# Low parts of weight tiles made by a negated copy on ScalarE and an adding DMA, in place of a subtraction on GpSimd

## What is computed

```python
def sq_relu_mlp(h, w_up, w_down):
    return jnp.square(jax.nn.relu(h @ w_up)) @ w_down

def swiglu(x, w_gate, w_up, w_down):
    return (jax.nn.silu(x @ w_gate) * (x @ w_up)) @ w_down
```

## Time and profile before

| | |
|---|---|
| time, median of 3 runs | 2312.11 us (2310.51 to 2312.12) |
| time of the profiled execution | 2310.62 us |
| its span | 2308.8 us |
| instructions | 29435 |
| granted TensorE clock | 0.999 |
| busy: PE, PEld | 99%, 82% of the span |
| busy: DVE, ACT, POOL | 46%, 44%, 58% |
| data moved by DMA | 213.74 MB, mean 93 GB/s |
| last chain, by engine | PE 91%, DVE 4%, POOL 2%, ACT 2%, issue 1% |

### The profile page before, as it was taken

The page is one execution under the profiler, slowest core; times in us unless marked ns, Lnnn a source line. Parts: engine busy times, 40 slices in busy tenths (PEclk is TensorE's granted clock), DMA queues, the critical chain, the costliest instruction groups (busy, mean ns, idle before and its releaser), DMA issues.

```text
span 2308.8 us, 29435 instructions
## 1 busy us (share of the span) xinstructions
PE 2287.9 (99%) x11249; PEld 1886.6 (82%) x11253; DVE 1064.7 (46%) x1428; ACT 1015.3 (44%) x1961; POOL 1335.8 (58%) x1008
## 2 busy tenths in 40 slices
PE   9999999999999999999999999999999999999998
PEld 8888888778878888788887888888898778888887
DVE  3423457544474656634546322434242564142534
ACT  4524444444674444443446233334333662333342
POOL 5533687783535778774354355768454503566773
PEclk9999999999999999999999999999999999999999
DMA  6321432322303243133330362331333202613222
GB/s 189 90 60 60 151 113 65 101 87 69 101 24 131 102 123 105 47 110 89 94 87 27 98 192 74 96 105 55 101 105 81 75 2 88 204 54 112 81 83 73
DMA packets 156947, 213.74 MB, mean 93 GB/s; under 512 B 33615, under 2 KB 81479, under 8 KB 156807
## 3 DMA queue, kind: packets, MB, share of 16 engines
q1 hardware_dynamic: 153424, 203.24, 29.4%
q10 hardware_dynamic: 3383, 8.62, 1.2%
HBM read 209.18 MB, written 2.10 MB: 92 GB/s over the span
## 4 chain that ended last, share of the span: by engine, by line
PE 91%; DVE 4%; POOL 2%; ACT 2%; issue 1%; DMA 0%; SPq 0%; DVEq 0%; ACTq 0%; POOLq 0%
PE PS L369 25%; PE PS L371 20%; PE PS L957 7%; PE PS L958 7%; PE PS L956 7%; PE PS L995 5%; PE PS L994 5%; PE PS L993 5%; PE PS L1944 2%; POOL WL L345 1%; PE PS L1922 1%; PE PS L489 1%; PE PS L2849 1%; DVE X L620 1%; ACT JUNK L578 1%
## 5 line engine op out<-in xcount | busy, mean ns | idle before, releaser
L345 POOL TENSOR_TENSOR WL<-WS,WH 128x512 fp32r<-128x512 f32 (+1 forms) x644 | 887.8, 1393 | 657.1 <-ACT WH L333 619.6
L333 ACT ACTIVATE WH<-WS 128x512 fp32r<-128x512 f32 (+2 forms) x606 | 373.8, 624 | 787.0 <-PE PS L369 283.2
L345 POOL TENSOR_TENSOR WL<-h_R,WH 128x512 fp32r<-128x512 f32 x240 | 348.6, 1473 | 115.1 <-ACT WH L330 112.2
L369 PE MATMUL PS<-AH,WH 128*128 128x512 f32 (+1 forms) x1072 | 324.0, 355 | 1.2 <-ACT AH L506 1.2
L369 PE MATMUL PS<-AL,WH 128*128 128x512 f32 (+1 forms) x1072 | 319.9, 352 | 0.5 <-DVE AL L524 0.3
L369 PE MATMUL PS<-AH,WL 128*128 128x512 f32 x880 | 313.2, 390 | 0.0
L956 PE MATMUL PS<-AH,WH 128*128 128x512 f32 x704 | 274.4, 390 | 0.6 <-POOL WL L345 0.6
L957 PE MATMUL PS<-AL,WH 128*128 128x512 f32 x704 | 274.6, 390 | 0.0
L958 PE MATMUL PS<-AH,WL 128*128 128x512 f32 x704 | 274.6, 390 | 0.0
L330 ACT ACTIVATE WH<-h_R 128x512 fp32r<-128x512 f32 x240 | 148.8, 631 | 244.3 <-PE PS L995 96.8
L371 PE MATMUL PS<-WH,AH 128*128 128x512 f32 (+1 forms) x552 | 214.9, 395 | 0.5 <-POOL WL L345 0.5
(11 more groups left out here) (419 smaller groups left out, 3647.1 us busy)
## 6 DMA issues: line engine op xcount, KB each, us to landing
WS<-in_mlp_w_up_dram SPq DMA_DIRECT2D x128, 256.0 KB, 3.1
h_R<-in_mlp_w_down_dram SPq DMA_DIRECT2D x96, 256.0 KB, 3.2
WS<-in_ffn_w_gate_dram SPq DMA_DIRECT2D x176, 128.0 KB, 2.2
WS<-in_ffn_w_up_dram SPq DMA_DIRECT2D x176, 128.0 KB, 2.2
h_R<-in_ffn_w_down_dram SPq DMA_DIRECT2D x64, 256.0 KB, 3.2
WS<-in_gla_w_in_dram SPq DMA_DIRECT2D x48, 256.0 KB, 2.7
WS<-in_even_w_in_dram SPq DMA_DIRECT2D x48, 256.0 KB, 2.6
WS<-in_mlp_w_down_dram SPq DMA_DIRECT2D x32, 256.0 KB, 2.8
```

The lines of the kernel that those rows point to most:

```text
L333: e.activation(WH[:, s, 0:n], WS[:, s, 0:n], ACT.Copy).then_inc(hi.sem, hi.tick(i))
L345: e.tensor_tensor(WL[:, s, 0:n], source, WH[:, s, 0:n].bitcast(F32), ALU.subtract).then_inc(lo.sem, lo.tick(i))
L369: return e.matmul(PS[b][0:mw, cs], weight[:, s, m * mw:(m + 1) * mw], x[:, cs], start=start, stop=stop, skip_group_check=head is not None)
```

## The change

For tiles of p1, p2 and p3 (`BY_DMA`) POOL no longer subtracts. ACT writes the tile twice: the rounded part into WH, and the same rounded part with a scale of -1 into WL. Then POOL, waiting for the second copy, issues a DMA that adds the raw tile in `hR` onto that slot of WL. Its landing is counted on one of six new semaphores (`rested`), and everybody who waited for `lo` of such a tile now waits for that: TensorE, SP's next load into the slot and its reload of the raw tile, and DVE where it overwrites a raw block or a WS slot. `rest(i)` picks the semaphore. The diff, with the places left out where only `w.wait_ge(lo, ...)` became `w.wait_ge(*rest(...))`:

```diff
+        rested = [Sig(ctx.enter_context(nc.semaphore(f"weight_rest_summed{i}"))) for i in range(NS)]
...
+        by_dma = set()
...
+        def rest(i):
+            return (rested[i % NS], i) if i in by_dma else (lo, i)
 
         def weight_in(e, w, i):
             if i >= len(stream):
                 return
             if i >= NS:
-                w.wait_ge(lo, i - NS)
+                w.wait_ge(*rest(i - NS))
...
                 source, *at = mixed[i]
                 w.wait_ge(*at)
                 e.activation(WH[:, s, 0:n], source, ACT.Copy).then_inc(hi.sem, hi.tick(i))
+                if i in by_dma:
+                    e.activation(WL[:, s, 0:n], source, ACT.Copy, scale=-1.0).then_inc(sc.sem, sc.tick("less", i))
                 return
...
             n, s = width(i), i % NS
+            if i in by_dma:
+                w.wait_ge(sc, "less", i)
+                e.dma_start(WL[:, s, 0:n], mixed[i][0], accum_op=ALU.add).then_inc(
+                    rested[s].sem, rested[s].tick(i, by=16))
+                return
             w.wait_ge(hi, i)
...
+        BY_DMA = ("p1", "p2", "p3")
...
             if c:
-                w.wait_ge(lo, first[D.name, c - 1, ("p4", "p5", "p2", "p3")[b]] + k)
+                w.wait_ge(*rest(first[D.name, c - 1, ("p4", "p5", "p2", "p3")[b]] + k))
...
                     mixed[i0 + k] = weight_source(D, c, p, k, i0 + k)
+                    if p in BY_DMA:
+                        by_dma.add(i0 + k)
...
                 s = (i0 + k) % NS
-                w.wait_ge(lo, i0 + k)
+                w.wait_ge(*rest(i0 + k))
```

More of the change, by code:

```diff
@@ L259, in program @@
         stored = Sig(ctx.enter_context(nc.semaphore("stored")))
-        sigs = [mm, sc, ve, po, hi, lo, stored, *landed, *ld.values(), *itertools.chain(*raw)]
+        sigs = [mm, sc, ve, po, hi, lo, stored, *landed, *rested, *ld.values(), *itertools.chain(*raw)]
         BA, BB = [0, 1, 2, 3], [4, 5, 6, 7]
@@ L409, in gemm @@
                 for kc in range(HEAD):
-                    w.wait_ge(lo, i0 + kc)
+                    w.wait_ge(*rest(i0 + kc))
                     for m in range(count(kc)):
@@ L462, in narrow @@
             i = first[name]
-            w.wait_ge(lo, i)
+            w.wait_ge(*rest(i))
             w.wait_ge(*held[b])
@@ L1059, in dve_weight_sums @@
                         ve.name("wsum", D.name, c, "p5", k)
-                        w.wait_ge(lo, first.get((D.name, c, "p1"), 0) + k)
+                        w.wait_ge(*rest(first.get((D.name, c, "p1"), 0) + k))
                     w.wait_ge(ve, "wsum", D.name, c, "p5", k0)
@@ L1069, in dve_weight_sums @@
                         w.wait_ge(raw[2][k], D.name, c)
-                        w.wait_ge(lo, first.get((D.name, c, "p6"), 0) + k)
+                        w.wait_ge(*rest(first.get((D.name, c, "p6"), 0) + k))
                     e.tensor_tensor(b11, b21, b11, ALU.subtract).then_inc(ve.sem, ve.tick())
```

## The result

The changed kernel takes 2323.22 us (median of 5 runs, 2321.59 to 2323.63) against 2312.11 us of the kernel before (2310.47 to 2312.20, 5 runs): 11.1 us more, ratio 1.0052 with a 95% interval of 1.0041 to 1.0062. It is slower, by more than twice the 0.2% that the prediction takes as what a measurement can tell apart.

The account below looks back on a forecast made before the run. TensorE was taken to bound the kernel. Narrow periods 6.8 us, less 0.5, plus 4.8 for wide adds meeting loads gave +11.1 us on 2310.6, said as 2322 us; range 2309 to 2350, the forecast's own 2316 to 2332.

Parts of the forecast that it names:

- TensorE bounds, the low parts have cover, and the narrow p2 and p3 are the thin place: TensorE idles only 20.9 us; low parts have 6 us of cover in wide periods, 1.1 to 1.9 in narrow runs.
- ACT's second copy costs nothing: On ACT: 120 scaled copies of 0.63 us, 76 us in all, fit its 0.75 us gaps; nothing paid.
- POOL's issue, 1.2 us taken: On POOL: 120 DMA issues of 1.2 us each; up to 1.4 us harmless, 2.0 the bad side.
- Rival 3: POOL's issue costs 2 us or more and paces the tiles: 20 us lost, 2331 us; chance 0.07.
- Pace of the adding DMA, 1.6 us a tile, against 1.386: In the DMA engines: an add takes 1.6 us a tile, lower bound 0.8, above TensorE's 1.386.
- Landing, 5.5 us taken from the 512 KB row: Adding DMA: 5.5 us from issue to landing, from a 5.0 us copy within SBUF plus 0.5; upper bound 9.3.
- rival 1: Not slower: add lands in about 4 us, pace at most 1.386 us; 2309 to 2314 us; chance 0.36, 0.04 faster.
- the narrow term: Narrow periods of both MLPs: adds late by 2.9 and 3.9 us, together 6.8, less about 0.5.
- Meeting with loads in the wide periods: Wide p2 and p3 of both MLPs: adds meet raw-tile loads, 0.6 us at each of 8, 4.8 us.
- SP's later loads cost nothing: On SP: loads wait for the landing and are asked for about 4 us later; costed at nothing.
- Rival 2: Adding DMA paced at 2.1 us a tile: 25 us, with loads 30, so 2342 us; chance 0.13.
- A cheaper POOL can give back at most 5.9 us: TensorE's waits for POOL's low parts total 5.9 us, 0.26%, the most that less POOL work can return.

Follow-up runs that it names:

- e1: Changed kernel without the adding DMA: ACT's second copy stays and POOL subtracts again after it; 2311.02 us, ratio 1.0000 to the kernel before.
- e7: Changed kernel with the DMA copying the raw tile into the low slot in place of adding it; 2312.42 us, ratio 1.0002 to the kernel before.
- e4: Changed kernel with loads of the next period's raw blocks 2 and 3 six tiles later in SP's queue; 2317.06 us, ratio 1.0026 to the kernel before.
- e6: Changed kernel with SP's loads waiting for an added tile's rounded part, not its add; 2328.60 us, ratio 1.0072 to the kernel before.
- e10: Changed kernel with the DMA making only p7's low parts in the narrow period, 8 tiles; 2304.91 us, ratio 0.9975 to the kernel before.
- e3: Changed kernel with p3 given back to POOL, p1 and p2 on the DMA; 2315.14 us, ratio 1.0017 to the kernel before.
- e9: Changed kernel with the adding DMA's destination named float32, so nothing is converted; 2322.46 us, ratio 1.0048 to the kernel before.
- e5: Changed kernel with POOL subtracting as before in the narrow period of each MLP; 2321.02 us, ratio 1.0039 to the kernel before.
- e11: Changed kernel with all seven products, 280 tiles in place of 120, on the DMA; 2334.32 us, ratio 1.0097 to the kernel before.
- e2: Changed kernel with only the 40 tiles of p1 on the DMA; 2311.39 us, ratio 1.0000 to the kernel before.
- e8: Changed kernel with raw blocks 2 and 3 loaded six tiles later and POOL subtracting in narrow periods; 2316.21 us, ratio 1.0016 to the kernel before.

## Why the prediction was right, step by step

It said 2322 us and a loss of 11.1 us by the profiled execution. Measured are 2323.22 us and 11.1 us between the medians, and the growth at the places of the adds is 10.8 us in the trace. The mechanism was right in the main: adds that land late behind full DMA engines, in the wide p3 and in the narrow runs. That the sum fits to 0.3 us or better is luck, since its two terms miss by 1.0 and 1.3 us in opposite directions, and for partly other reasons than those given.

- **TensorE bounds, the low parts have cover, and the narrow p2 and p3 are the thin place.** Right. p1 was never late, the SwiGLU networks lost nothing, as costed. But the longest wait of TensorE for an add, 1.7 us, stands in a wide p3 of mlp1, and not in the narrow periods, where the prediction looked for it.
- **ACT's second copy costs nothing.** Right (e1).
- **POOL's issue, 1.2 us taken.** It is 0.86 us in most cases, 0.93 in the mean. Rival 3 is out: the longest, 2.2 us, are issues queued on POOL that end 0.9 us apart, faster than TensorE's 1.386.
- **Pace of the adding DMA, 1.6 us a tile, against 1.386.** Right: 1.57 us. This term carried the sum. e7 shows that the addition is the cause of the loss; by the estimate given there the pace is the greater part of it.
- **Landing, 5.5 us taken from the 512 KB row.** Mis-sized as a fixed time: alone it is 3.2 to 3.5 us, and in company up to 9.5. The estimate of 3.2 us that the prediction worked out from the Trainium skill ("DMA: Bandwidth & Descriptors") agrees with the smallest landing in the trace, and adds in company are above it. Had the landing been 5.5 us by itself, the first tile of the narrow p2 would have been late in mlp0. It was not: 489.57 became 491.87, no more than the tiles ahead of it, and its add landed 3.4 us after the issue. By the prediction's own test ("It decides at 4.1 us from issue to landing") rival 1 should have come, so that test was wrong. The lateness came out at the last three tiles, where the adds met loads of up tiles, 2.1 us; the sum had 2.9, made of a landing that was 2.1 us too long and of no loads at all. The two errors nearly cancel. In mlp1 it was 2.9 (the sum had 3.9). Less the 0.5 taken off, the narrow term was 6.3 us, measured 5.0.
- **Meeting with loads in the wide periods, 0.6 us at each of eight products, 4.8 us.** The mechanism was right (e4), the places were not: nothing at p2 and 0.7 to 2.9 us at p3, 5.8 us. The overrun was worked out for 340 to 349 us, which is p3's stretch, and then spread over p2 as well. There is also a slip in the working: a third of 4.2 us less 0.6 us of spare is 0.8 us a product and not 0.6, which makes 6.4 us and a sum of 12.7.
- **SP's later loads cost nothing.** Right as a cost, but only half of it seen. ACT's waits for loads of the MLPs' up tiles went from 24.8 to 61.0 us, which the prediction had named as a sign of being wrong; they lay within cover, so they were no such sign, and the delay was of use (e6). DVE's waits ahead of p7 did not grow in all (16.6 us against 17.0), though the longest went from 2.4 to 4.9 us.
- **Rival 1** (not slower) needed a landing of about 4 us and a pace of at most 1.386. The first held for an add by itself, even for the first one of each narrow run (3.4 us). The second did not, and still less so beside loads. **Rival 2** needed 2.1 us a tile; it is 1.57.
- **"A cheaper POOL can give back at most 5.9 us".** The bound held (e10 gave 5.7), but I had dismissed it, since the waits follow DVE's sums. They do, and POOL's subtractions are what slows DVE. The rows for it stood in the earlier trace rows: 1211 ns at least and 2311 in the median for the same instruction.
- The half clock of 1.6 us was in no term. It is in the profile after and not in the one before. Since the times of the kernel before already fall near 2310.5 or near 2312.1 us, a profile of one that lies in the upper cluster may well have it too; no profile of that kernel here shows it, so how much of it is in the medians stays open.

What stays open: why mlp1 loses more at its second wide p3 (2.9 us) than the three others. The profile holds a candidate that no run tried. Every 13 to 37 us one packet of 16 KB of instructions takes one of the 16 DMA engines for 0.9 us or more, and the semaphore of an add, which counts to 16, is full only when the last engine is done. Such a packet starts at 936.7 us, within the last two adds of that p3, which land 8.5 and 9.5 us after their issue, the longest of all:

```profile
q8 instruction: 1, 0.02, 2.7%
...
DMA to landing us min/median/max: 6.4/8.5/9.5
```

(First row: the DMA queues in 936 to 938 us; second: L348 in 930 to 937.5 us.) Others start at 1000.7 us, at the narrow p2 of mlp1 that loses 1.3 us in one step, and in e3 at 839.1 us, for 2.35 us, at the wide p2 that grew unexpectedly. In e6 and e9 a packet of this kind is there as well and that wide p3 loses 1.2 and 1.8 us, so it can't be all. The wait of 1.4 to 2.7 us at the end of some of the programs was not tried either.

## What to carry to other kernels

Work that is taken off an idle engine and given to the DMA engines has to be counted there twice: as a latency against the cover of one tile, and as a pace against the consumer's, together with every load in the same stretch. An adding transfer within SBUF moved 256 KB in 1.57 us of all 16 engines, nearly twice a plain one, which is too slow for a consumer of 1.386 us even where each one lands in time, and the more so beside loads. And where one instruction shows two durations (1.2 and 2.3 us), look at what another engine does beside the long ones: worth moving here was the little that ran beside the late engine (8 tiles), not the whole class (120).

## What the runs showed of the hardware

- An adding DMA of 256 KB within SBUF, issued by POOL: 0.86 us of POOL, landing 3.2 us at least, 185 ns for a packet of 2 KB; the same without addition 0.53 us of POOL, 2.2 us at least and 99 ns. Naming the destination float32 changed nothing.
- DVE's sums of 128 x 1024 take 1.22 us beside POOL's DMA issues and 2.2 to 2.3 us beside its subtractions (e10 and before).
- TensorE's granted clock fell to 0.56 and 0.59 of 2.4 GHz over 4 us of 1752 to 1756 us, that is for most of it to the level of 1.2 GHz, with matmuls starting every 0.43 us in place of 0.23. Ahead of it TensorE had been busy without a gap in the projections of the odd mixer. The same place has it in e1, e3, e4, e5 and e9. In e6 and e11 a stretch like it is elsewhere, at 1001 to 1004 and 440 to 443 us, 0.2 and 1.0 us after the end of waits of TensorE of 1.84 and 2.69 us. The kernel before, e2, e7, e8 and e10 show none. So what TensorE did ahead of it differs, and these traces don't tell what brings it on. In the kernel after it costs 1.6 us, and less where TensorE would have waited anyway. The times of the kernel before fall into two clusters, near 2310.5 and 2312.1 us, and so do those of e1, whose profiled execution, 2312.0 us, has the half clock, where the one of the kernel before, 2310.6 us, has not. That fits, but one profile of each doesn't show it to be the cause.
- The end of a program can differ by 1.2 to 2.5 us behind its last store (0.2 us of waiting in most; 1.4 in e3, 2.1 in e11, 2.6 in e8, 2.7 in e5), with SP waiting for TensorE's queue.
